# Recurrent heads: gate products from high and low parts, their split behind the next head's evictions, one filling gate half moved ahead

## The chip, the core and the metric

The kernel runs on one core of a Trainium2 chip, in one launch. The metric is the device time of that launch in microseconds (us). Five engines run programs of their own, each strictly in its order, and meet through semaphores: TensorE (PE in the profile; PEld is its weight loading), VectorE (DVE), ScalarE (ACT), GpSimd (POOL) and SyncE (SP, which issues most loads).

## What is computed

The reference is two transformer-like blocks on 1024 positions of width 1024, in float32. The change concerns one part of the second block, the gated linear recurrence of `rglru_direction`, in ten heads of 128 channels:

```python
xa = depthwise_conv(u_a, conv_a_w[l], conv_a_b[l], LRU_CONV // 2)
h_fwd = rglru_direction(xa, wa_f[l], ba_f[l], wx_f[l], bx_f[l], lam_f[l], False)
h_bwd = rglru_direction(xa, wa_b[l], ba_b[l], wx_b[l], bx_b[l], lam_b[l], True)
...
def rglru_direction(xc, wa, ba, wx, bx, lam, reverse):
    r = jax.nn.sigmoid(block_diag(xc, wa, ba).astype(jnp.float32))
    i = jax.nn.sigmoid(block_diag(xc, wx, bx).astype(jnp.float32))
    log_a = -LRU_C * r * jax.nn.softplus(-lam.astype(jnp.float32))
    a = jnp.exp(log_a)
    b_in = jnp.sqrt(-jnp.expm1(2.0 * log_a)) * (i * x32)
    _, h = lax.associative_scan(_lin_combine, (a, b_in), axis=1, reverse=reverse)
```

`block_diag` is block-diagonal: each head has its own 128x128 matrix, for each of four gates (r and i, forward and backward). So a head needs four products of a 128x128 matrix with its 128x1024 channels.

## The kernel before

Nearly all large products are made from split operands: a float32 matrix is written as a high part (ScalarE's copy to the 32-bit type fp32r) and a low part (the matrix less its high part, by GpSimd or VectorE), and three matmuls of such parts stand for one float32 product (the helper `three`, lines 401 to 403, which add hi*hi, hi*lo and lo*hi into one bank). Weights come in tiles of 128x1024: SP loads one into one of three staging buffers, ScalarE writes `weight_hi` (line 439), GpSimd `weight_lo` (line 461); five tiles are held at a time, and a tile's slot is filled again as soon as its last use is issued (`o.released()`).

There is no scheduler. One list of steps is written by hand (`order_lru` for this part), and each engine's program is that list, less the steps in which it has no part. So the place of a step in the list sets its place in the queue of each engine that takes part.

The recurrent heads run one behind the other, j from 0 to 9. For each j the list holds, in this order:

- `front(j + 1)` for the next head: `head_load` (SP loads the four matrices into `wbd`), `u` twice (24 matmuls of the projection each; ScalarE evicts each half into `raw`), a weight split for the slot that came free, `head_conv` (ScalarE's first tap, line 2661, then three taps on VectorE, line 2668, giving `xc`).
- `head_gate` eight times: TensorE multiplies `wbd` and `xc` in plain float32 (line 2681), ScalarE evicts with a sigmoid into `gt` (line 2692).
- `head_decay` for both directions: ScalarE's exponential `dc` and tanh `th` (lines 2701 and 2702), which read `gt`.
- `head_mid`: GpSimd squares `dc` (line 2708, called a2 below) and multiplies `gt` by `xc` (2710); VectorE makes `th` from a2 (2717, 2719).
- `gates.fill(1)`: one half (128x512, 24 matmuls) of the block's output gates, which have no bond to the heads and fill TensorE's time; ScalarE evicts it (line 854).
- `head_scan`: ScalarE's square root (2725), VectorE's product and scan for each direction (2732, 2740, 2742), into `hs`.
- `head_sum`: GpSimd adds both directions (2749) and issues the store (2751).
- `gates.fill(1)`: a second half, after which one more weight tile is split.

For the last head `window_front(0)`, the first projection of the pooling branch, stands in place of `front`. The pooling stage follows (`pool_out`, line 2834).

Of the kernel before, what the change touches and what calls it, by code (L numbers as in the profile page):

```python
# [7 lines left out]
F32 = mybir.dt.float32  # L8
F32R = mybir.dt.float32r
I32 = mybir.dt.int32  # L10
ALU = mybir.AluOpType
# [3 lines left out]
P = 128  # L15
# [162 lines left out]
class Memory:  # L178
# [5 lines left out]
    def put(self, name, shape, dtype=F32, right=False):  # L184
        n = int(np.prod(shape[1:])) * 4
        n = (n + 31) // 32 * 32
        self.names += 1
        if right:
            self.hi -= n
            at = self.hi  # L190
        else:
            at = self.lo
            self.lo += n
        assert self.lo <= self.hi, (name, self.lo, self.hi)
        return self.nc.alloc_sbuf_tensor_at(f"{name}_{self.names}", shape, dtype, offset=at)
# [203 lines left out]
def three(q, out, stat, mov, first, final, onto=False):  # L399

    q.matmul(out, stat[0], mov[0], start=first, stop=False, skip_group_check=onto)  # L401
    q.matmul(out, stat[0], mov[1], start=False, stop=False, skip_group_check=onto)  # L402
    return q.matmul(out, stat[1], mov[0], start=False, stop=final, skip_group_check=onto)  # L403
# [2272 lines left out]
def pe_head_gate(K, j, i, h):  # L2676
    pe, S, key = K.pe, K.S, ("lru", j, i, h)
    b = K.open(key)
    pe.wait_ge(S.wbd_load[j % 2], j)
    pe.wait_ge(S.dve_op, ("xc", j))  # L2680
    pe.q.matmul(b, K.wbd[j % 2][:, i, :], K.xc[j % 2][:, h * HALF:(h + 1) * HALF], start=True, stop=True).then_inc(*S.mm.up(key))


def act_head_gate(K, j, i, h):
# [219 lines left out]
def lay_out(K):  # L2904
# [80 lines left out]
            K.br[2] = [pair("br", [P, NL, HALF]), pair("br", [P, NP, HALF])]  # L2985
    m.lo, m.hi = end, high
    xn = [put("xn", [P, D], right=True) for _ in range(2)]
    below_xn = m.hi
    hT2 = pair("hT", [P, ND, S], right=True)

    m.lo, m.hi = low, below_xn
# [65 lines left out]
    m.lo = gates2_end  # L3057
    K.hs, K.xc = [put("hs", [P, S]) for _ in range(2)], [put("xc", [P, S]) for _ in range(2)]
    K.raw, K.raw2 = put("raw", [P, 16 + S + 16]), put("raw2", [P, 16 + S + 16])
    K.wbd, K.wpool = [put("wbd", [P, 4, P]) for _ in range(2)], put("wpool", [P, 2, GDIM])  # L3060
    K.sums = [put("sums", [P, 16 + S + 16]) for _ in range(2)]
    K.counts, K.pooled, K.yb2 = K.gt[0], K.dc, K.th

    K.norms = {
# [900 lines left out]
def order_lru(o, mix_norm):  # L3965
    gates = Gating(o, "gates2")
    gates.open()

    def block(c):
        w = o.take(gates.tile(c))  # L3970
        for h in range(NHALF):
            gates.one(c, h, w)
            yield
    blocks = [block(c) for c in range(GATES_AHEAD)]
    for n, b in enumerate(blocks):
        next(b)
        advance(mix_norm, (3, 0, 2, 0)[n])
    finish(mix_norm)
    for b in blocks:
        finish(b)  # L3980
    gates.done = 2 * GATES_AHEAD
    gates.close()
    o.handover()
    o.do("x2_stored")
    o.do("rates")
    gates.open()
    o.do("lru_edges")

    def front(j):
        o.do("head_load", j)  # L3990
        w = o.take(weight_block(o.io["w_in_2"][0], j * P))
        for h in range(NHALF):
            o.do("u", j, w, h)
        o.released()
        o.do("head_conv", j)
    def window_front(c):
        w = o.take(weight_block(o.io["w_in_2"][0], LW + c * P))
        for h in range(NHALF):
            o.do("pool_u", c, w, h)
        o.released()  # L4000
    front(0)
    for j in range(NL):
        if j + 1 < NL:
            front(j + 1)
        else:
            window_front(0)
        for i in range(4):
            for h in range(NHALF):
                o.do("head_gate", j, i, h)
        for d in range(2):  # L4010
            o.do("head_decay", j, d)
        for d in range(2):
            o.do("head_mid", j, d)
        gates.fill(1)
        for d in range(2):
            o.do("head_scan", j, d)
        o.do("head_sum", j)
        gates.fill(1)
    o.do("ya_stored")
    o.do("pool_edges")  # L4020
    for g in range(len(WINDOWS)):
        last = g + 1 == len(WINDOWS)
        if g == 0:
            o.do("counts_load", 0)
            o.do("wpool_load", 0)
            o.do("window_sums", 0)
            o.do("window_mean", 0)
            window_front(1)
            o.do("window_sums", 1)
            o.do("window_mean", 1)  # L4030
        if last:
            o.do("branch_fetch", 2, 0, 0, 0, NL)
            o.do("branch_fetch", 2, 0, 1, 0, NP - 2)
        gates.fill(2 * POOL_GATES[g])
        if last:
            gates.close()
            o.handover()
            for k in range(6):
                o.do("branch_load", 2, 0, 0, k)
        else:  # L4040
            window_front(2 * g + 2)
            o.do("counts_load", g + 1)
            window_front(2 * g + 3)
            o.do("window_sums", 2 * g + 2)
        for blk in (2 * g, 2 * g + 1):
            for h in range(NHALF):
                o.do("pool_out", blk, h)
            if not last:
                o.do("pool_store", blk)
        if not last:  # L4050
            o.do("wpool_load", g + 1)
            o.do("window_mean", 2 * g + 2)
            o.do("window_sums", 2 * g + 3)
            o.do("window_mean", 2 * g + 3)
    for k in range(6, NL):
        o.do("branch_load", 2, 0, 0, k)
    for k in range(NP):
        o.do("branch_load", 2, 0, 1, k)
    for blk in range(NP - 2, NP):
        o.do("pool_store", blk)  # L4060
# [44 lines left out]
def scalar_program(K, steps):  # L4105
    part = {"x_load": act_x_load, "square_in": act_square_in, "param": act_param, "weight": act_weight,
            "rstd": act_rstd, "turn": act_turn, "handover": act_handover, "gate": act_gate,
            "gates_close": act_gates_close, "z": act_z, "lora": act_lora, "sig_g": act_sig_g, "prep_kk": act_prep_kk,
            "prep_lora": act_prep_lora, "prep_decay": act_prep_decay, "prep_scale": act_prep_scale,
            "prep_length": act_prep_length, "tok": act_tok, "first": act_first, "level_w": act_level_w,  # L4110
            "local": act_local, "solve": act_solve, "bring": act_bring, "second": act_second, "compact": act_compact, "state": act_state, "y_turn": act_y_turn, "finish_1": act_finish_1,
            "finish_3": act_finish_3, "finish_4": act_finish_4, "compressed": act_compressed, "cnorm": act_cnorm, "cturn": act_cturn,
            "angles": act_angles, "q": act_q, "kv": act_kv, "exponent": act_exponent, "turn_p": act_turn_p,
            "output": act_output, "branch_load": act_branch_load, "gate_sum": act_gate_sum,
            "merge_rows": act_merge_rows, "split_hi": act_split_hi, "join": act_join,
            "act_split": act_act_split, "raw_first": act_raw_first, "conv_first": act_conv_first, "gelu": act_gelu, "down_rows": act_down_rows,
            "store_rows": act_store_rows, "ple_mix": act_ple_mix, "x2_stored": act_x2_stored, "rates": act_rates,
            "lru_edges": act_lru_edges, "u": act_u, "head_conv": act_head_conv, "head_gate": act_head_gate,
            "head_decay": act_head_decay, "head_scan": act_head_scan, "ya_stored": act_ya_stored,
            "pool_u": act_pool_u, "pool_store": act_pool_store, "yb_stored": act_yb_stored}  # L4120
    for kind, *what in steps:
        if kind in part:
            part[kind](K, *what)
# [21 lines left out]


def gpsimd_program(K, steps):
    part = {"param_load": pool_param_load, "param": pool_param, "weight": pool_weight, "gain": pool_gain,
            "handover": pool_handover, "gates_close": pool_gates_close, "rwkv_ready": pool_rwkv_ready,
            "level": pool_level,  # L4150
            "finish_4": pool_finish_4, "branch_load": pool_branch_load, "gate_sum": pool_gate_sum,
            "parts": pool_parts, "split_lo": pool_split_lo, "act_split": pool_act_split, "x2_stored": pool_x2_stored, "head_mid": pool_head_mid,
            "head_sum": pool_head_sum, "ya_stored": pool_windows_begin, "yb_stored": pool_yb_stored}
    for kind, *what in steps:
        if kind in part:
            part[kind](K, *what)
# [65 lines left out]
```

## Time and profile before

| what | value |
|---|---|
| median of 3 runs | 3463.3 us (3461.95 to 3465.99) |
| profiled execution | 3459.81 us, its span 3458.5 us |
| mean granted TensorE clock | 0.993 of full speed |
| PE busy | 3346.1 us, 97% of the span |
| DVE, ACT, POOL busy | 59%, 40%, 38% of the span |

The profile is of one execution. Its span is what the trace covers, and the time of that execution is 1.3 us longer. An engine's busy share is an average over all stages; the stage of the heads lies between 2046 and 2360 us of the span. A busy PE is one with some matmul in flight, and one matmul's duration in a row contains time that overlaps the next one; the distance between starts tells the rate.

### The profile page before, as it was taken

Reading aid. Unit: us, or ns where it says so; the run is one execution under the profiler, and the core shown is the slowest. Engines: PE = TensorE matmul, PEld = TensorE weight load, DVE = VectorE, ACT = ScalarE, POOL = GpSimd, SP = SyncE. Lnnn points to the kernel's source line nnn. Section 1 sums busy time; section 2 is a strip of 40 time slices with the busy share of each in tenths; the row PEclk is TensorE's granted clock in tenths of the full one; section 3 lists DMA queues with packets and bytes.
Section 4 is the critical chain, followed back from the end, with each engine's and each line's share of the span. In section 5 each row is a group of like instructions: output and inputs, shape, how many; then the busy total and the mean of one; then the engine's idle time right before and its main releaser. Section 6 shows DMA issues by size and latency. Waiting matters only on the chain.

```text
span 3458.5 us, 48890 instructions
## 1 busy us (share of the span) xinstructions
PE 3346.1 (97%) x19926; PEld 2718.4 (79%) x19926; DVE 2044.4 (59%) x2689; ACT 1390.3 (40%) x2361; POOL 1318.8 (38%) x698
## 2 busy tenths in 40 slices
PE   7999999999989999999999999999999999999999
PEld 6788888897668778878887777777788877777787
DVE  3655737427754743345555538886544588888554
ACT  4443434344533544431114447772233343443212
POOL 3212222110024444444442116662344365666542
PEclk9999999999999999999999999999999999999999
DMA  5101111020036344452222322222465423333522
GB/s 155 41 19 47 42 33 48 26 62 8 1 106 214 110 140 143 134 182 98 95 95 91 109 86 77 84 84 100 163 203 166 142 82 106 112 108 108 184 96 81
DMA packets 343792, 344.40 MB, mean 100 GB/s; under 512 B 14662, under 2 KB 263938, under 8 KB 343569
## 3 DMA queue, kind: packets, MB, share of 16 engines
q1 hardware_dynamic: 328960, 307.00, 28.1%
q10 hardware_dynamic: 11520, 25.17, 1.9%
q0 software_dynamic: 3088, 9.10, 0.7%
q8 instruction: 159, 2.61, 0.3%
q14 instruction: 65, 0.52, 0.1%
HBM read 268.86 MB, written 72.35 MB: 99 GB/s over the span
## 4 chain that ended last, share of the span: by engine, by line


## 5 line engine op out<-in xcount | busy, mean ns | idle before, releaser
L461 POOL TENSOR_TENSOR weight_lo<-stage,weight_hi 128x1024 fp32r<-128x1024 f32 (+4 forms) x269 | 627.9, 2341 | 981.5 <-ACT weight_hi L439 952.7
L2459 DVE TENSOR_TENSOR x<-x,psum 128x512 f32<-128x512 f32 x416 | 283.9, 687 | 281.7 <-PE psum L403 271.2
L439 ACT ACTIVATE weight_hi<-stage 128x1024 fp32r<-128x1024 f32 (+4 forms) x329 | 299.6, 925 | 328.5 <-PE psum L403 285.2
L401 PE MATMUL psum<-hT_hi,weight_hi 128*128 128x512 f32 x1024 | 411.0, 401 | 1.5 <-DVE hT_lo L654 1.5
L402 PE MATMUL psum<-hT_lo,weight_hi 128*128 128x512 f32 x1024 | 400.1, 391 | 0.0
L403 PE MATMUL psum<-hT_hi,weight_lo 128*128 128x512 f32 x1024 | 399.7, 390 | 0.0
L401 PE MATMUL psum<-weight_hi,act_hi 128*128 128x512 f32 x864 | 337.1, 390 | 5.3 <-POOL act_lo L2407 4.2
L403 PE MATMUL psum<-weight_hi,act_lo 128*128 128x512 f32 x864 | 336.9, 390 | 0.0
L402 PE MATMUL psum<-weight_lo,act_hi 128*128 128x512 f32 x864 | 336.8, 390 | 0.0
L461 POOL TENSOR_TENSOR weight_lo<-sum,weight_hi 128x512 fp32r<-128x512 f32 (+1 forms) x114 | 238.3, 2100 | 233.8 <-ACT weight_hi L439 233.7
L401 PE MATMUL psum<-T_hi,weight_hi 128*128 128x512 f32 x608 | 238.5, 392 | 18.5 <-POOL weight_lo L461 14.5
L402 PE MATMUL psum<-T_lo,weight_hi 128*128 128x512 f32 x608 | 236.7, 389 | 0.0
L403 PE MATMUL psum<-T_hi,weight_lo 128*128 128x512 f32 x608 | 236.7, 389 | 0.0
L401 PEld LDWEIGHTS psum<-hT_hi,weight_hi 128*128 128x128 f32 x1024 | 193.2, 189 | 50.6 <-issue 5.5
L402 PEld LDWEIGHTS psum<-hT_lo,weight_hi 128*128 128x128 f32 x1024 | 193.4, 189 | 43.0 <-issue 4.3
L403 PEld LDWEIGHTS psum<-hT_hi,weight_lo 128*128 128x128 f32 x1024 | 193.0, 188 | 40.8
L401 PEld LDWEIGHTS psum<-weight_hi,act_hi 128*128 128x128 f32 x864 | 162.6, 188 | 39.9 <-ACT out L2300 2.5
L2407 POOL TENSOR_TENSOR act_lo<-act_raw,act_hi 128x1024 fp32r<-128x1024 f32 x54 | 131.7, 2460 | 153.1 <-ACT act_hi L2398 153.1
L403 PEld LDWEIGHTS psum<-weight_hi,act_lo 128*128 128x128 f32 x864 | 162.6, 188 | 34.1
L402 PEld LDWEIGHTS psum<-weight_lo,act_hi 128*128 128x128 f32 x864 | 162.5, 188 | 33.8
L401 PE MATMUL psum<-B_hi,weight_hi 128*128 128x512 f32 x456 | 179.9, 394 | 8.1 <-ACT kept L2289 3.7
L402 PE MATMUL psum<-B_lo,weight_hi 128*128 128x512 f32 x456 | 178.8, 392 | 0.0
(421 smaller groups left out, 7095.5 us busy)
## 6 DMA issues: line engine op xcount, KB each, us to landing
stage<-in_w_up SPq DMA_DIRECT2D x66, 512.0 KB, 4.3
stage<-in_w_in SPq DMA_DIRECT2D x64, 512.0 KB, 4.0
act_raw<-scratch_act SPq DMA_DIRECT2D x54, 512.0 KB, 5.3
stage<-in_w_ffn_up SPq DMA_DIRECT2D x48, 512.0 KB, 4.7
scratch_gates<-gate ACTq DMA_DIRECT2D x64, 256.0 KB, 2.0
gs<-scratch_gates SPq DMA_DIRECT2D x64, 256.0 KB, 3.1
stage<-in_w_out SPq DMA_DIRECT2D x32, 512.0 KB, 4.5
scratch_act<-out SPq DMA_DIRECT2D x64, 256.0 KB, 4.8
```

The costliest lines, as they stand in the source:

```text
L401: q.matmul(out, stat[0], mov[0], start=first, stop=False, skip_group_check=onto)
L402: q.matmul(out, stat[0], mov[1], start=False, stop=False, skip_group_check=onto)
L403: return q.matmul(out, stat[1], mov[0], start=False, stop=final, skip_group_check=onto)
L439: a.q.activation(hi[:, part], src, ACT.Copy).then_inc(*S.w_hi.up(w))
L461: g.q.tensor_tensor(lo[:, part], src, hi[:, part].bitcast(F32), ALU.subtract).then_inc(*S.w_lo_pool.up(w))
L2407: g.q.tensor_tensor(lo, K.act_raw[i % 4][:, :], hi.bitcast(F32), ALU.subtract).then_inc(*S.act_lo.up((f, i)))
L2459: v.q.tensor_tensor(dst, dst, K.bank(key), ALU.add).then_inc(*S.x.up(("f", f, g, t, n)))
```

## The change

The gate products are made by `three` from `wbd_hi`, `wbd_lo`, `xc_hi` and `xc_lo`. A new step `head_split` makes these: ScalarE copies `xc` and `wbd` to the high parts, GpSimd subtracts for the low parts. The step for head j stands in `front(j + 1)`, behind the weight split and ahead of `head_conv`. The `fill` that stood behind `head_mid` stands ahead of the gates.

```diff
 def pe_head_gate(K, j, i, h):
     pe, S, key = K.pe, K.S, ("lru", j, i, h)
     b = K.open(key)
-    pe.wait_ge(S.wbd_load[j % 2], j)
-    pe.wait_ge(S.dve_op, ("xc", j))
-    pe.q.matmul(b, K.wbd[j % 2][:, i, :], K.xc[j % 2][:, h * HALF:(h + 1) * HALF], start=True, stop=True).then_inc(*S.mm.up(key))
+    pe.wait_ge(S.act_op, ("wbd_hi", j))
+    pe.wait_ge(S.pool_op, ("wbd_lo", j))
+    at = slice(h * HALF, (h + 1) * HALF)
+    three(pe.q, b, (K.wbd_hi[:, i, :], K.wbd_lo[j % 2][:, i, :]), (K.xc_hi[:, at], K.xc_lo[:, at]), True, True).then_inc(*S.mm.up(key))
+
+
+def act_head_split(K, j):
+    a, S = K.a, K.S
+    a.wait_ge(S.dve_op, ("xc", j))
+    if j:
+        a.wait_ge(S.mm, ("lru", j - 1, 3, 1))
+    a.q.activation(K.xc_hi[:, :], K.xc[j % 2][:, :], ACT.Copy).then_inc(*S.act_op.up(("xc_hi", j)))
+    a.wait_ge(S.wbd_load[j % 2], j)
+    a.q.activation(K.wbd_hi[:, :, :], K.wbd[j % 2][:, :, :], ACT.Copy).then_inc(*S.act_op.up(("wbd_hi", j)))
+
+
+def pool_head_split(K, j):
+    g, S = K.g, K.S
+    g.wait_ge(S.act_op, ("xc_hi", j))
+    g.q.tensor_tensor(K.xc_lo[:, :], K.xc[j % 2][:, :], K.xc_hi[:, :].bitcast(F32), ALU.subtract).then_inc(*S.pool_op.up(("xc_lo", j)))
+    g.wait_ge(S.act_op, ("wbd_hi", j))
+    g.q.tensor_tensor(K.wbd_lo[j % 2][:, :, :], K.wbd[j % 2][:, :, :], K.wbd_hi[:, :, :].bitcast(F32), ALU.subtract).then_inc(
+        *S.pool_op.up(("wbd_lo", j)))
...
         for h in range(NHALF):
             o.do("u", j, w, h)
         o.released()
+        if j:
+            o.do("head_split", j - 1)
         o.do("head_conv", j)
...
             front(j + 1)
         else:
             window_front(0)
+            o.do("head_split", j)
+        gates.fill(1)
         for i in range(4):
...
         for d in range(2):
             o.do("head_mid", j, d)
-        gates.fill(1)
         for d in range(2):
             o.do("head_scan", j, d)
```

`wbd_lo` lies in place over `wbd`; `xc_hi`, `xc_lo` and `wbd_hi` get room of their own.

Where the new instructions land is shown at two places. First GpSimd's queue over one head in steady state, before: the sum of the head just ended, its store, two weight splits, then the four operations of the next head's `head_mid`.

```order
L2749 TENSOR_TENSOR hs_258<-hs_258,hs_259 128x1024
L2751 DMA scratch_ya<-hs_258 128x1024
L461 TENSOR_TENSOR weight_lo_66<-stage_52,weight_hi_65 128x1024
L461 TENSOR_TENSOR weight_lo_62<-stage_53,weight_hi_61 128x1024
L2708 TENSOR_TENSOR gt_248<-dc_252 128x1024
L2710 TENSOR_TENSOR gt_249<-gt_249,xc_261 128x1024
L2708 TENSOR_TENSOR gt_250<-dc_253 128x1024
L2710 TENSOR_TENSOR gt_251<-gt_251,xc_261 128x1024
```

The same stretch of GpSimd's queue with the change:

```order
L2769 TENSOR_TENSOR hs_258<-hs_258,hs_259 128x1024
L2771 DMA scratch_ya<-hs_258 128x1024
L461 TENSOR_TENSOR weight_lo_66<-stage_52,weight_hi_65 128x1024
L461 TENSOR_TENSOR weight_lo_62<-stage_53,weight_hi_61 128x1024
L2698 TENSOR_TENSOR xc_lo_271<-xc_261,xc_hi_270 128x1024
L2700 TENSOR_TENSOR wbd_lo_273<-wbd_265,wbd_hi_269 128x512
L2728 TENSOR_TENSOR gt_248<-dc_252 128x1024
L2730 TENSOR_TENSOR gt_249<-gt_249,xc_261 128x1024
L2728 TENSOR_TENSOR gt_250<-dc_253 128x1024
L2730 TENSOR_TENSOR gt_251<-gt_251,xc_261 128x1024
```

The two subtractions of the new step stand behind the sum of the head before and the two weight splits, and ahead of the squares that need this head's gates.

The other place is ScalarE's queue between two heads, with its waits, with the change (before, the two rows at lines 2690 and 2692 and the two of the filling gate, 854 and 859, are not between `weight_hi` and the gates' sigmoids).

```order
L439 ACTIVATE weight_hi_61<-stage_53 128x1024 [waits stage_load1]
L2690 ACTIVATE xc_hi_270<-xc_261 128x1024
L2692 ACTIVATE wbd_hi_269<-wbd_265 128x512 [waits wbd_load1]
L2661 ACTIVATE xc_260<-raw_262,param_50 128x1024 [waits pool_op_done,act_evac_done]
L854 ACTIVATE gate_246<-psum,param_50 128x512 [waits gates2_store0,mm_done]
L859 DMA scratch_gates<-gate_246 128x512 [waits gate_ready]
L2712 ACTIVATE gt_248<-psum,param_50 128x512 [waits mm_done] x2
```

ScalarE makes the next head's first tap (line 2661) later by the two copies, and one of its two filling evictions has moved ahead of the sigmoids. On TensorE the eight gate products of a head, 8 float32 matmuls before, are 24 matmuls of parts, and 24 matmuls of a filling half stand ahead of them and no longer behind them.

## Rows read from the trace of the kernel before

**Rows 1.** Windows: PE, PEld, DVE, ACT, POOL busy us; clock; DMA share; GB/s.
```profile
2150.00:2180.00 30.00, 30.00 (x117) 21.64 (x116) 26.79 (x12) 23.00 (x27) 19.88 (x9) 1.00 0.25 79
```
**Rows 2.** Timeline of PE: start us, us, then idle before. First head's gates.
```profile
2029.77 0.39 PE L401 MATMUL psum<-hT_hi,weight_hi 128*128 128x512 f32 x1
...
2062.18 0.39 PE L403 MATMUL psum<-hT_hi,weight_lo 128*128 128x512 f32 x1
2062.41 7.03 PE L2681 MATMUL psum<-xc,wbd 128*128 128x512 f32 x16
...
2069.50 0.39 PE L402 MATMUL psum<-hT_lo,weight_hi 128*128 128x512 f32 x1
```
**Rows 3.** Timeline of PE's weight loads: first of the gates of two heads.
```profile
2119.48 0.41 PEld L2681 LDWEIGHTS psum<-xc,wbd 128*128 128x128 f32 x2
...
2148.12 0.41 PEld L2681 LDWEIGHTS psum<-xc,wbd 128*128 128x128 f32 x2
```
**Rows 4.** Timeline of POOL: first head's weight split, then one steady head.
```profile
2064.33 2.35 POOL L461 TENSOR_TENSOR weight_lo<-stage,weight_hi 128x1024 fp32r<-128x1024 f32 x1 [5.92 <-ACT weight_hi L439]
...
2151.02 2.35 POOL L2749 TENSOR_TENSOR hs<-hs,hs 128x1024 f32<-128x1024 f32 x1 [8.79 <-DVE hs L2742]
...
2154.28 5.77 POOL L461 TENSOR_TENSOR weight_lo<-stage,weight_hi 128x1024 fp32r<-128x1024 f32 x2
2160.00 2.89 POOL L2708 TENSOR_TENSOR gt<-dc 128x1024 f32<-128x1024 f32 x1
...
2179.66 2.36 POOL L2749 TENSOR_TENSOR hs<-hs,hs 128x1024 f32<-128x1024 f32 x1 [8.79 <-DVE hs L2742]
```
**Rows 5.** Timeline of DVE: second head's taps, then a steady head's.
```profile
2065.49 4.92 DVE L2668 SCALAR_TENSOR_TENSOR xc<-raw,param,xc 128x1024 f32<-128x1024 f32 x3 [3.35 <-ACT xc L2661]
...
2151.68 9.46 DVE L2668 SCALAR_TENSOR_TENSOR xc<-raw,param,xc 128x1024 f32<-128x1024 f32 x3 [0.74 <-ACT xc L2661]
2162.99 3.33 DVE L2717 SCALAR_TENSOR_TENSOR th<-gt,th 128x1024 f32<-128x1024 f32 x1 [1.85 <-POOL gt L2708]
```
**Rows 6.** Timeline of ACT: last square root of a head, next head's tanh.
```profile
2172.72 1.06 ACT L2725 ACTIVATE th<-th 128x1024 f32<-128x1024 f32 x1 [3.01 <-DVE th L2719]
...
2187.29 1.14 ACT L2702 ACTIVATE th<-gt,neg 128x1024 f32<-128x1024 f32 x1
```
**Rows 7.** Timelines of PE, ACT and POOL in the last head.
```profile
2320.18 7.03 PE L2681 MATMUL psum<-xc,wbd 128*128 128x512 f32 x16
...
2327.25 0.69 ACT L2692 ACTIVATE gt<-psum,param 128x512 f32<-128x512 f32 x1 [0.17 <-PE psum L2681]
...
2331.52 1.90 POOL L2708 TENSOR_TENSOR gt<-dc 128x1024 f32<-128x1024 f32 x1 [0.60 <-ACT th L2702]
...
2350.20 2.40 POOL L2749 TENSOR_TENSOR hs<-hs,hs 128x1024 f32<-128x1024 f32 x1 [8.79 <-DVE hs L2742]
```
**Rows 8.** Groups by line and shape from 1500 us on: subtractions and a copy.
```profile
L461 POOL TENSOR_TENSOR weight_lo<-stage,weight_hi 128x512 fp32r<-128x512 f32 x22 | 48.2, 2193 | 0.0
L2080 POOL TENSOR_TENSOR merged_lo<-gs,merged_hi 128x512 fp32r<-128x512 f32 x16 | 20.7, 1297 | 121.9 <-ACT merged_hi L2073 121.9
...
L439 ACT ACTIVATE weight_hi<-stage 128x1024 fp32r<-128x1024 f32 x155 | 162.2, 1054 | 289.3 <-PE psum L403 269.2 <-DMA stage<-in_w_out 6.9 <-ACT gate L854 5.6
```
**Rows 9.** PE and PEld behind an idle stretch, and its clock by stretches.
```profile
2473.45 0.47 PE L401 MATMUL psum<-br_hi,weight_hi 128*128 128x512 f32 x1 [2.08 <-DVE br_lo L2025]
...
2475.71 0.33 PEld L403 LDWEIGHTS psum<-br_hi,weight_lo 128*128 128x128 f32 x1
2476.14 0.33 PEld L401 LDWEIGHTS psum<-br_hi,weight_hi 128*128 128x128 f32 x1
...
2475.00:2476.00 1.00, 1.00 (x3) 0.80 (x3) 1.00 (x1) 0.00 (x0) 1.00 (x1) 0.50 1.05 412
...
2478.00:2479.00 1.00, 1.00 (x6) 0.83 (x5) 1.00 (x3) 0.00 (x0) 0.34 (x1) 1.00 0.06 25
```
**Rows 10.** Timeline of PE at the pooling stage's first products.
```profile
2371.39 7.11 PE L2834 MATMUL psum<-dc,wpool 128*128 128x512 f32 x16 [0.65 <-DVE dc L2825]
```

More of the change, by code:

```diff
@@ L2987, in lay_out @@
     xn = [put("xn", [P, D], right=True) for _ in range(2)]
-    below_xn = m.hi
+    below_xn = xn_at = m.hi
     hT2 = pair("hT", [P, ND, S], right=True)
@@ L3059, in lay_out @@
     K.raw, K.raw2 = put("raw", [P, 16 + S + 16]), put("raw2", [P, 16 + S + 16])
+    wbd_at = m.lo
     K.wbd, K.wpool = [put("wbd", [P, 4, P]) for _ in range(2)], put("wpool", [P, 2, GDIM])
     K.sums = [put("sums", [P, 16 + S + 16]) for _ in range(2)]
+    K.wbd_hi = put("wbd_hi", [P, 4, P], F32R)
+    assert m.lo <= lows_at
+    m.lo = xn_at
+    K.xc_hi, K.xc_lo = put("xc_hi", [P, S], F32R), put("xc_lo", [P, S], F32R)
+    m.lo = wbd_at
+    K.wbd_lo = [put("wbd_lo", [P, 4, P], F32R) for _ in range(2)]
     K.counts, K.pooled, K.yb2 = K.gt[0], K.dc, K.th
@@ L4117, in scalar_program @@
             "store_rows": act_store_rows, "ple_mix": act_ple_mix, "x2_stored": act_x2_stored, "rates": act_rates,
-            "lru_edges": act_lru_edges, "u": act_u, "head_conv": act_head_conv, "head_gate": act_head_gate,
+            "lru_edges": act_lru_edges, "u": act_u, "head_conv": act_head_conv, "head_gate": act_head_gate, "head_split": act_head_split,
             "head_decay": act_head_decay, "head_scan": act_head_scan, "ya_stored": act_ya_stored,
@@ L4147, in gpsimd_program @@
 def gpsimd_program(K, steps):
-    part = {"param_load": pool_param_load, "param": pool_param, "weight": pool_weight, "gain": pool_gain,
+    part = {"head_split": pool_head_split, "param_load": pool_param_load, "param": pool_param, "weight": pool_weight, "gain": pool_gain,
             "handover": pool_handover, "gates_close": pool_gates_close, "rwkv_ready": pool_rwkv_ready,
```

## The prediction

> **What bounds the kernel now.** I first read the windows of the heads' stage: TensorE is busy for all of 30.00 us at full clock, and VectorE, ScalarE and GpSimd for 26.8, 23.0 and 19.9 us of it [rows 1]. Three engines that are this full beside a full TensorE call for a second look: who waits for whom. The timeline of TensorE shows an unbroken stream. Ahead of the first gates 144 matmuls of parts start between 2029.77 and 2062.18, 0.2266 us apart, and the 16 records of eight float32 products last from 2062.41 until the filling half's second matmul at 2069.50; less that half's first matmul, 6.86 us [rows 2]. The gates of the next heads begin 28.64 us apart [rows 3]. That is just TensorE's work for one head: 6.86 us, and 96 matmuls of parts (two halves of a projection, two filling halves) in 21.75 us.
>
> The timelines of the other engines show a second bound of the same length, and it is the one that matters here. GpSimd starts a head's sum when VectorE's last scan has ended, stores, splits two weight tiles from 2154.28 and comes to the next head's a2 at 2160.00; its next sum starts at 2179.66, 28.64 us after the one before, and its only long wait is 8.79 us for the scan [rows 4]. VectorE's first work on a2 starts at 2162.99, released by GpSimd [rows 5]. From a2 on VectorE works without a gap to the scan, and the scan lets the next sum start. So scan, sum, weight splits, a2, scan is a closed chain without slack. What keeps it at 28.64 us is that the head's gates are not in it: ScalarE has this head's tanh at 2187.29 + 1.14 = 2188.43, just before GpSimd needs it, since TensorE made the gates while the previous head was still in its scans [rows 6].
>
> **What the change takes away.** Eight float32 products of 6.86 us become 24 matmuls of parts at 0.2266 us, 5.44 us: 1.42 us a head, 14.2 us over ten. TensorE's work for a head falls to 27.2 us.
>
> **What it adds, and where.** ScalarE gets a 128x1024 copy (1.05 us by the weights' copy) and one of 128x512, some 0.6 us as half of it and a fixed part [rows 8]. They lie behind the projection's evictions; GpSimd is then still waiting for the scan or splitting weights, so they cost nothing by themselves. If that cover went, they would cost 1.7 us a head. GpSimd gets xc_lo (128x1024) and wbd_lo (128x512). Their price alone would be small. Their place is not: in GpSimd's queue they stand behind the previous head's sum and behind both weight splits, and ahead of a2. The gates wait for wbd_lo, a2 waits for the gates. What ran beside the previous head's scans, the gates and their evictions, now starts only after them. The order of one head becomes a single chain, which I add up from one start of the gates to the next:
>
> - 24 matmuls: 23 x 0.2266 us and the last one's 0.39 us make 5.6 us [rows 2]; at the clock that I expect, 1.6 us more (below): 7.2 us.
> - Last eviction to a2: in the last head, where nothing else stood in the way, the eviction began at 2327.25 and a2 at 2331.52, 4.27 us; with a hop from TensorE, 4.3 us [rows 7]. All eight evictions stand ahead of the tanh in ScalarE's queue, so the whole set of gates is in the chain.
> - a2 to the sum: 2331.52 to 2350.20, 18.7 us [rows 7].
> - Sum to the weight splits: 2151.02 to 2154.28, 3.3 us [rows 4].
> - Two weight splits and xc_lo: the two took 5.72 us (2154.28 to 2160.00) while VectorE's taps ran; at that rate three take 8.6 us [rows 4].
> - wbd_lo: between 1.30 and 2.19 us by the two rows of 128x512 subtractions [rows 8]. By then the three taps, of some 3 us each beside the splits [rows 5], are over; I take 1.3 us, and 0.1 us for hops: 1.4 us.
>
> Together 43.5 us where there were 28.64. TensorE has 27.2 us of work in it at full clock and idles for about 14 us in each head. The filling half ahead of the gates doesn't cover this: the wait is longer than all the other work that a head has.
>
> **The clock.** Such waits have a price of their own. TensorE resumed at 2473.45 after an idle stretch of 2.08 us; in 2475 to 2476 the granted clock was 0.50 of full speed, the 1.2 GHz level, with weight loads 0.43 us apart in place of 0.23, and from 2478 it was 1.00 [rows 9]. So I expect the first gates of each head at half speed. From 2475 to 2478 about 3 us were slow; with the partly slow ends I take 3.4 us, in which 8 matmuls run where 15 would: 7 x 0.2266 = 1.6 us. The bounds are none, and the whole set at 0.43 us, 4.7 us.
>
> The Trainium skill, page "TensorE: Matmul & The Clock Gate", section "HAM oscillation — how this bites in real kernels", describes this: a loop that leaves TensorE waiting in every turn starts every turn at the low clock. The trace agrees with its one such wait (0.50 after 2.08 us); by the page alone each turn would start slowly, which the sum already holds.
>
> **Blocking between VectorE and GpSimd.** Three taps took 4.92 us when GpSimd had little to do and 9.46 us beside its splits [rows 5], and two splits took 5.72 us instead of 2 x 2.35 us [rows 4]. This is in the 8.6 us above. Without it three would take 7.05 us.
>
> The Trainium skill, page "SBUF — State Buffer", section "Who interferes with whom", has a stricter rule: a two-input VectorE operation and a GpSimd operation that reads SBUF exclude each other for a whole instruction. If VectorE were first each time, xc_lo and each split would wait for a tap of about 1.3 us; the three would take about 11 us and the kernel some 20 us more than I forecast. The split's 2.86 us beside the taps shows about 0.5 us each, so I stay with the row.
>
> **The ends.** First head: GpSimd ends a weight split at 2064.33 + 2.35 = 2066.68 [rows 4]; xc_lo (2.9 us beside the next head's taps) and wbd_lo (1.3 us) end near 2071.0, where the gates began at 2062.41 [rows 2]: 8.6 us late, 5.4 us of them spent on the filling half. Last head: no taps beside the splits, so 7.1 us in place of 8.6, and the turn is 42.0 us. The last gates come later by 8.6 + 8 x (43.5 - 28.64) + (42.0 - 28.64) = 140.9 us. Behind them the chain to the pooling products is as long as before, to 0.2 us (7.2 + 4.3 = 11.5 us to a2, before 2331.52 - 2320.18 = 11.3) [rows 7]. TensorE waited 0.65 us there [rows 10]; now it has 5.4 us less to fill the time, waits some 6 us and meets the low clock once more, 1.6 us. Sum: 142.7 us.
>
> On the profiled execution that is 3459.8 + 142.7 = 3602.5 us; the median of the runs lay 3.5 us above it, so I forecast 3605 us for a median. About 0.2% is what a measurement of this kernel can tell from no change.
>
> **Rivals.**
>
> - *A single chain (the forecast)*: chance 82%. With no slow clock, no blocking and the low price of wbd_lo the turn is 40.3 us and the kernel about 3575 us; with all gates at the low clock and 2.2 us for wbd_lo, 47.4 us and about 3644 us.
> - *GpSimd has room* (the other side): its 8.79 us of waiting in each head would hold both subtractions (some 4.2 us), TensorE would stay full, and the 14.2 us would be gained: 3449 us. This decides if wbd_lo comes within the 21.75 us of other matmuls between two sets of gates. For it speaks that GpSimd is 38% busy. Against it: the 8.79 us lie ahead of the sum, the subtractions behind it. 4%.
> - *Only GpSimd's chain grows*: the two subtractions lengthen the old chain by some 4.2 us a head, and the gates still overlap the scans: ten times 4.2 us on the median, 3505 us. It would need a2 not to depend on late gates, and it reads `dc`, made from them. 5%.
> - *The low clock stays*: TensorE is granted its lower level for most of each turn. The gates then cost 10.3 us, and the other 96 matmuls 41 us, more than the chain leaves them, so that TensorE would bound a turn of about 51 us: some 3680 us. Rows 9's recovery within about 3 us of work speaks against it, since 22 us of work lie unbroken behind the gates. 6%.
> - *No change to speak of*: the gain and some waits cancel. 3%.
>
> **How the numbers follow.** The forecast is the first case. Its bounds, a little widened at the low end, give 3570 to 3645 us, which leaves the other cases, 18%, outside. Faster by over 0.2%: 4%. Within 0.2%: 3%. Slower: 93%.
>
> **What would show it.** In the changed profile the gates should start about 43 us apart, with TensorE idle for some 14 us ahead of them, released by GpSimd's `wbd_lo`; the clock should be at its low level at their start; GpSimd should go from the sum through two splits and two subtractions without a gap, and then wait about 11 us for the tanh. DVE and ACT should have the same work a head, spread thinner. I am wrong if TensorE stays full in this stage, if the wait ends with another engine, or if the starts are under 38 us apart.

## The result and the profile after

| what | before | changed |
|---|---|---|
| median, us (runs) | 3462.7 (4) | 3609.1 (4), 3607.7 to 3611.4 |
| ratio to before | 1 | 1.0424, 95% interval 1.0410 to 1.0439 |
| profiled execution, us | 3459.8 | 3611.4, its span 3610.1 |
| mean granted TensorE clock | 0.993 | 0.970 |

The change costs 146 us; the forecast was 3605 us, 4 us less than was measured, inside 3570 to 3645. The table of waits of the changed kernel (us in total, times, longest) shows the place in one line, the first of TensorE's list:

```profile
PE psum L401 <- POOL wbd_lo L2700: 134.4, 10, 14.8
```

Windows of the same kernel (columns as in [rows 1]) show what became of TensorE's unbroken stream, and the granted clock at the start of one head's gates:

```profile
2180.00:2210.00 30.00, 15.22 (x61) 12.21 (x60) 20.73 (x10) 11.32 (x14) 17.41 (x8) 0.73 0.25 79
...
2206.00:2207.00 1.00, 0.34 (x1) 0.37 (x2) 0.00 (x0) 0.00 (x0) 0.52 (x1) 0.50 0.00 0
2210.00:2211.00 1.00, 1.00 (x3) 0.78 (x3) 0.00 (x0) 0.41 (x2) 0.00 (x0) 0.50 0.00 0
2211.00:2212.00 1.00, 1.00 (x5) 0.76 (x4) 0.00 (x0) 0.82 (x2) 0.00 (x0) 0.96 0.00 0
2212.00:2213.00 1.00, 1.00 (x6) 0.84 (x5) 0.00 (x0) 1.00 (x2) 0.00 (x0) 1.00 0.00 0
```

TensorE is busy for 15.2 of 30 us where [rows 1] had 30.0, and no other engine is full in its place: VectorE, ScalarE and GpSimd all do less in the stretch than before. That is how a chain looks, in contrast to a busy engine that sets the pace.

One turn of the chain, from the timelines of all engines in the changed kernel, in order of time:

```profile
2162.36 0.29 PEld L401 LDWEIGHTS psum<-xc_hi,wbd_hi 128*128 128x128 f32 x1 [15.17 <-issue]
...
2174.44 1.89 POOL L2728 TENSOR_TENSOR gt<-dc 128x1024 f32<-128x1024 f32 x1 [12.19 <-ACT th L2722]
...
2193.11 2.35 POOL L2769 TENSOR_TENSOR hs<-hs,hs 128x1024 f32<-128x1024 f32 x1 [8.79 <-DVE hs L2762]
2195.23 1.31 DVE L2668 SCALAR_TENSOR_TENSOR xc<-raw,param,xc 128x1024 f32<-128x1024 f32 x1 [2.20 <-ACT xc L2661]
2196.38 5.64 POOL L461 TENSOR_TENSOR weight_lo<-stage,weight_hi 128x1024 fp32r<-128x1024 f32 x2
2201.98 3.31 POOL L2698 TENSOR_TENSOR xc_lo<-xc,xc_hi 128x1024 fp32r<-128x1024 f32 x1
2205.26 1.26 POOL L2700 TENSOR_TENSOR wbd_lo<-wbd,wbd_hi 128x512 fp32r<-128x512 f32 x1
2206.63 0.29 PEld L401 LDWEIGHTS psum<-xc_hi,wbd_hi 128*128 128x128 f32 x1 [15.17 <-issue]
2206.66 0.77 PE L401 MATMUL psum<-xc_hi,wbd_hi 128*128 128x512 f32 x1 [14.78 <-POOL wbd_lo L2700]
2207.23 0.63 PE L402 MATMUL psum<-xc_lo,wbd_hi 128*128 128x512 f32 x1
...
2208.32 0.69 ACT L2712 ACTIVATE gt<-psum,param 128x512 f32<-128x512 f32 x1 [12.54 <-PE psum L403]
...
2520.86 4.49 PE L2854 MATMUL psum<-dc,wpool 128*128 128x512 f32 x5 [4.81 <-DVE dc L2845]
```

Read down the left column: gates at 2162.36, a2 at 2174.44, sum at 2193.11, splits at 2196.38 to 2206.5, the next gates at 2206.63. GpSimd's, TensorE's and ScalarE's steps in this list follow one another; only VectorE's tap (line 2668) runs beside a split. GpSimd waits 12.19 us for the tanh, where before its only long wait was the one for the scan [rows 4]; ScalarE waits 12.54 us for the gates' first bank. The last row is the pooling product that answers to [rows 10]: its wait grew from 0.65 to 4.81 us.

### The profile page after: what moved, and what is told of

Same layout as the page of the kernel before. It is cut to its first block, busy times and chain, and to the rows that moved or that the text cites. A ratio compares the mean times of both kernels' runs of the same rounds, so it can differ in the third digit from the quotient of the medians.

```text
span 3610.1 us, 49080 instructions
## 1 busy us (share of the span) xinstructions
PE 3359.1 (93%) x20006; PEld 2750.9 (76%) x20006; DVE 2040.1 (57%) x2689; ACT 1398.5 (39%) x2371; POOL 1353.0 (37%) x718
## 4 chain that ended last, share of the span: by engine, by line
```

## The experiments

All medians stand beside runs of the kernel before on the same chip; those gave medians of 3462.5 to 3462.9 us. "A turn" is the distance between the starts of two heads' gates, by the weight loads: 28.64 us before, 44.3 us in the changed kernel.

### One part alone

**e2_fill_ahead_alone**, the kernel before with only the filling half moved:

```diff
+        gates.fill(1)
         for i in range(4):
...
             o.do("head_mid", j, d)
-        gates.fill(1)
```

> The kernel before with only the filling half moved ahead of the float32 gates; no split. Single chain: the gates need nothing from the previous head's scan, so TensorE stays full in the heads and the turn is 28.6 to 29.5 us; the tail lacks 5.4 us of filling work: 3466 to 3480 us. Rival (the half's new place is what slows the changed kernel): most of the 146 us, 3560 us or more.

3469.1 us, ratio 1.0018 (1.0008 to 1.0028). Turns stay at 28.64 us; TensorE waits 5.0 us at the pooling products, since one half fewer lies behind the last gates. This part is worth 6 us of the 146.

**e5_split_unread**, the changed kernel with the gates in plain float32 again. The split is made, but nothing reads it, so that TensorE doesn't wait for it; `wbd_lo` no longer lies over `wbd` but in the room of a later stage's buffer (an edit not shown here):

```diff
-    pe.wait_ge(S.pool_op, ("wbd_lo", j))
...
-    three(pe.q, b, (K.wbd_hi[:, i, :], K.wbd_lo[j % 2][:, i, :]), (K.xc_hi[:, at], K.xc_lo[:, at]), True, True).then_inc(*S.mm.up(key))
+    pe.wait_ge(S.wbd_load[j % 2], j)
+    pe.wait_ge(S.dve_op, ("xc", j))
+    pe.q.matmul(b, K.wbd[j % 2][:, i, :], K.xc[j % 2][:, h * HALF:(h + 1) * HALF], start=True, stop=True).then_inc(*S.mm.up(key))
```

> The changed kernel's order with the split made in its place but not read: the gates are the float32 products of before (wbd_lo is written to a buffer of the later pooling stage). Single chain: with the gates out of it, only GpSimd's two subtractions lengthen the old chain of 28.65 us, to about 33 us a turn; with the moved half's 6 us at the end 3500 to 3515 us. So of the 146 us about 40 would be GpSimd's extra work and the rest the gates' wait for it. Rival (GpSimd's extra work alone is what costs): 3590 us or more. Rival (GpSimd has room): 3469 us, as with the half moved alone.

3500.6 us, ratio 1.0113 (1.0097 to 1.0130). One turn is 32.3 us by GpSimd's a2:

```profile
2212.56 1.92 POOL L2727 TENSOR_TENSOR gt<-dc 128x1024 f32<-128x1024 f32 x1
...
2244.85 1.91 POOL L2727 TENSOR_TENSOR gt<-dc 128x1024 f32<-128x1024 f32 x1
```

That is the old chain, longer by the two subtractions. TensorE's own 28.64 us a head, with the float32 gates, lie below it and don't set the pace. So 38 us of the 146 are the extra work in GpSimd's queue and the moved half; the other 108 us come only from the gates' waiting for it. This is the division that the forecast and its rival "only GpSimd's chain grows" (3505 us) disputed.

**e1_fill_back**, the changed kernel with the half behind `head_mid` again (the diff of e2 turned round):

> The changed kernel with the filling gate half back behind head_mid; the split stays where the change put it. Single chain (scan, sum, two weight splits, xc_lo, wbd_lo, gates, tanh, a2, scan): the filling half isn't in that chain, so the gates stay 44.3 us apart and TensorE's wait ahead of them grows from 14.8 to about 20 us; only the tail, where the half fills TensorE's 4.8 us again, gives some back: 3600 to 3611 us. Rival (the moved half delays each head's gates by its 5.4 us): 39 us a turn, about 3555 us.

3594.3 us, ratio 1.0373 (1.0358 to 1.0389): 15 us faster than the changed kernel, neither what I expected nor the rival's figure. TensorE still waits 123.9 us for `wbd_lo`, and a turn is 42.3 us on average. The difference is in the timelines of VectorE and GpSimd:

```profile
2187.81 9.53 DVE L2668 SCALAR_TENSOR_TENSOR xc<-raw,param,xc 128x1024 f32<-128x1024 f32 x1 [3.05 <-ACT xc L2661]
2188.10 4.64 POOL L461 TENSOR_TENSOR weight_lo<-stage,weight_hi 128x1024 fp32r<-128x1024 f32 x2
2192.70 2.34 POOL L2698 TENSOR_TENSOR xc_lo<-xc,xc_hi 128x1024 fp32r<-128x1024 f32 x1
2195.00 1.25 POOL L2700 TENSOR_TENSOR wbd_lo<-wbd,wbd_hi 128x512 fp32r<-128x512 f32 x1
```

One tap lasts 9.53 us, from 0.29 us ahead of GpSimd's first split until 1.1 us behind its last subtraction, where in the changed kernel the tap that starts 1.15 us ahead of the split took 1.31 us. Here VectorE stands still and GpSimd's three large subtractions take 6.98 us by their rows, not 8.95 as in the changed kernel. VectorE is not in the chain at that time, GpSimd is: so 2 us a turn are gained by which of the two comes first (from the first split to the gates it is 8.26 us in each of e1's turns, 10.25 in the changed kernel's first eight).

### The clock

**e4_keep_warm** and **e8_warm_later_heads** put useless matmuls, whose result nothing reads, ahead of the filling half's own, in all heads and in heads 1 to 9:

```diff
-        gates.fill(1)
+        gates.fill(1, 20)                 # e4: 20 x 3 more matmuls
...
+        gates.fill(1, 20 if j else 0)     # e8
```

> The changed kernel with 60 useless matmuls (13.6 us at full clock) ahead of the filling half that precedes each head's gates; they write a bank that the half then overwrites. Single chain: TensorE's wait ahead of the gates shrinks from 14.8 to about 1 us, the gates then run at full clock, and the turn falls from 44.3 to about 42.1 us: 3585 to 3595 us, faster than the changed kernel in spite of 136 us of added work. Rival (the low clock costs nothing in the chain): 3605 to 3611 us. Rival (TensorE's own work bounds the heads): 3745 us.

> The useless matmuls ahead of the filling half only for heads 1 to 9, not for head 0, where TensorE has no long wait for them to fill. If the low clock costs about 1.8 us a turn and head 0 paid some 11 us for its useless matmuls: 3590 to 3596 us. If the clock is not what the useless matmuls changed: 3603 us or more.

e4 took 3603.7 us (ratio 1.0405, 1.0390 to 1.0421), e8 3594.0 us (1.0382, 1.0367 to 1.0398); the mean granted clock was 0.993 in both. e4 missed because head 0 has no long wait to fill: its gates began at 2083.9 in place of 2074.4. In e8 turns are 42.5 us against 44.3: from the gates to a2 it is 10.07 us in place of some 12.1, and the three splits with their hop take 0.2 us more (10.42 against 10.25). The low clock therefore costs some 2 us a turn, of which 1.8 us come back in e8, 15 us in all, a tenth of the loss.

### The split at another place

**e3_split_early** makes head j+1's split behind `head_mid` of head j, ahead of the previous sum in GpSimd's queue (and the half at its old place), so that the new step no longer stands behind that sum:

```diff
-            o.do("head_split", j - 1)
...
             o.do("head_mid", j, d)
+        if j + 1 < NL:
+            o.do("head_split", j + 1)
+        gates.fill(1)
```

**e7_split_at_scans** puts it behind `head_scan`, **e6_weights_deferred** is e3 with the two weight splits behind that split too (`o.released(2)` there; none behind the projections).

> Gate products from parts, but head j+1's split stands right behind head j's head_mid, ahead of the sum of head j and of the weight splits; the filling half is back behind it. Single chain: the split falls into GpSimd's wait for the scans (8.8 us), the gates again run beside the scans; the turn is bound by the old chain of 28.65 us with some blocking on VectorE, 28.6 to 29.8 us: 3460 to 3477 us, TensorE at full clock. Rival (the price of GpSimd's extra work, wherever it stands): 4.5 us a head more, about 3508 us. Rival (TensorE's saving counts now): 3449 us.

> The early split moved a little later, from behind head_mid to behind head_scan (still ahead of the sum): GpSimd then subtracts beside VectorE's scans and no longer beside its maximum and first product. If the 3.2 us a turn that the early split cost came from blocking of those operations, most of it goes and the turn is 28.7 to 30 us: 3463 to 3480 us. If the scans are blocked as well, 31 to 32.5 us: 3490 to 3510 us.

> The early split (right behind head_mid), and the two weight splits of a head also moved from behind the sum to behind that split. Chain: scan, sum, a2 no longer holds the 5.7 us of weight splits, so the turn is bound by TensorE's 27.2 us if the weight splits fit beside VectorE's work: 3449 us. Rival (GpSimd and VectorE exclude each other, and the weight splits now fall on VectorE's chain from a2 to the scan): 28.5 to 31 us a turn, 3463 to 3490 us.

| | median, us | ratio (95%) | steady turn, us |
|---|---|---|---|
| e3 | 3499.6 | 1.0105 (1.0090 to 1.0120) | 31.8 |
| e7 | 3500.6 | 1.0114 (1.0099 to 1.0129) | 31.8 |
| e6 | 3497.6 | 1.0104 (1.0089 to 1.0119) | 31.3 |

The place of the split is what mattered: each is over 100 us faster than the changed kernel. But all three stop 35 to 38 us above the kernel before, wherever GpSimd's work stands. Of e3's theories the forecast (3460 to 3477 us) failed; nearest was the rival by which the work costs 4.5 us a head wherever it stands (3508 us), where 3.2 us a turn were measured. e7 came out as its second theory had it, with the scans blocked as well (3490 to 3510 us). e6 is above both of its theories. VectorE's timeline in e3, where GpSimd's two subtractions run from 2219.82 to 2224.85 and nothing of GpSimd from there to 2231.78:

```profile
2211.97 3.34 DVE L2737 SCALAR_TENSOR_TENSOR th<-gt,th 128x1024 f32<-128x1024 f32 x1 [4.22 <-POOL gt L2728]
...
2220.98 2.75 DVE L2739 TENSOR_SCALAR th<-th 128x1024 f32<-128x1024 f32 x1
2223.65 2.28 DVE L2752 TENSOR_TENSOR th<-th,gt 128x1024 f32<-128x1024 f32 x1
2225.97 2.29 DVE L2760 TENSOR_TENSOR_SCAN hs<-dc,th 128x1024 f32<-128x1024 f32 x1
2228.18 1.20 DVE L2752 TENSOR_TENSOR th<-th,gt 128x1024 f32<-128x1024 f32 x1
2229.42 2.29 DVE L2762 TENSOR_TENSOR_SCAN hs<-dc,th 128x1024 f32<-128x1024 f32 x1
```

Timelines of VectorE and GpSimd in e6:

```profile
2219.25 2.72 DVE L2739 TENSOR_SCALAR th<-th 128x1024 f32<-128x1024 f32 x1
...
2223.05 7.72 POOL L461 TENSOR_TENSOR weight_lo<-stage,weight_hi 128x1024 fp32r<-128x1024 f32 x2
2224.22 4.36 DVE L2760 TENSOR_TENSOR_SCAN hs<-dc,th 128x1024 f32<-128x1024 f32 x1
2228.50 3.36 DVE L2752 TENSOR_TENSOR th<-th,gt 128x1024 f32<-128x1024 f32 x1
```

and in e7:

```profile
2195.05 3.52 POOL L2698 TENSOR_TENSOR xc_lo<-xc,xc_hi 128x1024 fp32r<-128x1024 f32 x1 [3.93 <-ACT xc_hi L2690]
2196.30 3.35 DVE L2752 TENSOR_TENSOR th<-th,gt 128x1024 f32<-128x1024 f32 x1
2198.53 2.25 POOL L2700 TENSOR_TENSOR wbd_lo<-wbd,wbd_hi 128x512 fp32r<-128x512 f32 x1
2199.69 3.24 DVE L2762 TENSOR_TENSOR_SCAN hs<-dc,th 128x1024 f32<-128x1024 f32 x1
...
2224.01 0.69 DVE L2739 TENSOR_SCALAR th<-th 128x1024 f32<-128x1024 f32 x1
```

The same operations last 0.69 us (L2739), 1.20 us (L2752) and 2.29 us (the scan) when GpSimd does nothing. Beside a subtraction each grows by 1 to 2 us, and GpSimd's subtractions grow too (two in 7.72 us, 4.64 us alone in e1). So the two engines hold each other off, and much of VectorE's busy time is not work.

What bounds the turn is not the same in the three. In e3 and e7 VectorE still has a gap of 4.22 us in each turn, ended by a2: the old chain through sum, weight splits and a2 is still closed there, and longer by what its operations lose beside the subtractions. In e6 VectorE has no gap for a whole turn. Counted by the shortest time of each in that run, a turn's operations are 14.6 us on VectorE and 19.7 us on GpSimd; their sum, an estimate of 34 us, is a little above the turn of 31.3 us, so that hardly any of it overlaps. In e6 the sum of both is what comes near the bound.

### Room for GpSimd

If that is so, taking work off GpSimd must help. ScalarE can square `dc`:

```diff
+    a.wait_ge(S.act_op, ("tanh", j, d))
+    a.q.activation(K.gt[2 * d][:, :], K.dc[d][:, :], ACT.Square).then_inc(*S.act_op.up(("a2", j, d)))
...
-    g.q.tensor_tensor(K.gt[2 * d][:, :], K.dc[d][:, :], K.dc[d][:, :], ALU.mult).then_inc(*S.pool_op.up(("a2", j, d)))
```

**e10_square_act_alone** is this edit on the kernel before, **e9_early_square_act** on e3, **e11_deferred_square_act** on e6. **e12_both_full** is e11 with two steps moved: head 0's split to behind its own `front`, and the filling half ahead of the gates for heads 0 to 8, which saves ScalarE one 1.28 us change between its sets of functions a head.

> The kernel before, with a2 by ScalarE and nothing else. TensorE's float32 gates keep its turn at 28.64 us, so nothing is gained: 3458 to 3468 us. If the chain of the other engines was the only bound before: 3450 us or less.

> The early split, and a2 (the square of dc) by ScalarE in place of GpSimd. If VectorE and GpSimd exclude each other so far that the sum of their work bounds the turn of 31.8 us of the early split, 3.8 us less on GpSimd give 27.5 to 29 us a turn: 3450 to 3468 us. If instead GpSimd's order (sum, weight splits, then head_mid) is the bound: the turn loses only what stood between the splits and VectorE's first work, about 2 us: 29.8 us, 3470 to 3485 us. If ScalarE becomes the bound by its two squares: 31 us or more, 3490 us.

> The early split with the weight splits behind it, and a2 by ScalarE. If the sum of VectorE's and GpSimd's work bounds the turn (31.3 us with a2 on GpSimd), 3.8 us less give 27.3 to 28.5 us: 3449 to 3463 us. If ScalarE's chain (square root, next gates, tanh, squares) becomes the bound: 29 us or more, 3466 us or more.

> The kernel of the run before (weights' splits deferred, square on ScalarE) with the filling half ahead of the gates again in heads 0 to 8 and with head 0's split ahead of head 1's front. Its mean turn was 28.1 us by the starts of the gates, its best turns 27.20 us, TensorE's own work for a head; its last turns were 28.2 us, where ScalarE's queue closed a chain of its own, and head 0 cost 6.5 us of waiting for wbd_lo. With the filling half's eviction standing ahead of the sigmoids ScalarE changes between its sets of functions once less in a head, 1.28 us less work a turn. Theory that ScalarE's chain was the last bound: all turns come to 27.2 us, head 0 waits little, and of the 14.2 us that TensorE saves some 5 to 12 us appear: 3450 to 3458 us, faster than both kernels. Rival, VectorE and GpSimd with their mutual exclusion are the bound by now whatever ScalarE does: turns stay at 28 us or go above, and the time is 3460 us or more.

| | median, us (11 runs each) | ratio (95%) | turns, us |
|---|---|---|---|
| e10 | 3461.8 | 0.9996 (0.9987 to 1.0005) | 28.64 |
| e9 | 3462.8 | 0.9999 (0.9990 to 1.0008) | 28.9, then 27.2 to 28.4 |
| e11 | 3463.9 | 1.0004 (0.9995 to 1.0013) | 29.8, then 27.2 to 27.3, the last two 28.2 |
| e12 | 3461.0 | 0.9996 (0.9987 to 1.0005) | 27.2, one 27.8, the last 25.6 (no half ahead of its gates) |

On the kernel before, the square's move does nothing (e10: TensorE is the bound as well). On e3 and e6 it takes 34 to 37 us away. On e3 the move also takes a2 out of the closed chain, so that e9 alone doesn't tell the chain from the sum; e11, made from e6, is the test of the sum. (e11's nine turns are 27.7 us on average, not 28.1 as the expectation of e12 has it.) In e12 TensorE has its full stream again at the 27.2 us of work that the change leaves it, and even so the kernel is no faster than before by what a measurement can tell. Of the 12.8 us that nine shorter turns should bring, 8.8 are left at the last gates and 4.9 at the pooling products. Windows, then VectorE and GpSimd in the last head, then TensorE at the last gates and at the pooling products, of e12:

```profile
2200.00:2230.00 30.00, 30.00 (x134) 24.85 (x133) 29.72 (x13) 25.06 (x29) 24.01 (x10) 1.00 0.25 79
```

```profile
2329.29 2.42 POOL L461 TENSOR_TENSOR weight_lo<-stage,weight_hi 128x1024 fp32r<-128x1024 f32 x1
2329.55 10.30 DVE L2736 SCALAR_TENSOR_TENSOR th<-gt,th 128x1024 f32<-128x1024 f32 x1 [3.67 <-ACT gt L2724]
2331.66 4.75 POOL L2730 TENSOR_TENSOR gt<-gt,xc 128x1024 f32<-128x1024 f32 x2
2336.39 2.38 POOL L461 TENSOR_TENSOR weight_lo<-stage,weight_hi 128x1024 fp32r<-128x1024 f32 x1
```

```profile
2314.28 0.47 PE L401 MATMUL psum<-xc_hi,wbd_hi 128*128 128x512 f32 x1 [1.48 <-POOL wbd_lo L2700]
...
2369.39 1.19 PE L2853 MATMUL psum<-dc,wpool 128*128 128x512 f32 x1 [4.72 <-DVE dc L2844]
```

VectorE is at 29.72 of 30 us (30.1 us of operations in a turn of 27.2, counted as above). The last gates start at 2314.28, after a wait of 1.5 us for `wbd_lo` and 5.9 us before [rows 7]'s 2320.18, or 8.8 us if one allows for the 2.9 us by which this execution was late ahead of the stage (its weight split of [rows 4]'s time comes at 2058.91, in the profile of before at 2056.01). Then one product of VectorE lasts 10.30 us, until GpSimd's four operations are done; the pooling products start at 2369.4, only 4.9 us earlier by the same allowance. TensorE has run out of work 4.7 us before that, and meets the lower level (0.50 in the windows from 2369 to 2374). What is left is 1.5 us of the median, inside its uncertainty. e12's theory was right for the turns and wrong for the time.

The Trainium skill, page "SBUF — State Buffer", section "Who interferes with whom", says that a two-input VectorE operation and a GpSimd operation that reads SBUF exclude each other for a whole instruction, and that the order of issue decides who is blocked. On the exclusion the 9.53 and 10.30 us rows agree, and there the loser waits for four GpSimd operations in a row. On the order the rows don't decide: in e1 the tap that lost began 0.29 us ahead of the split.

## Why the prediction was right

- **The mechanism** held: gates, a2, scans, sum, splits, gates is one chain, TensorE waits in every head (13.4 us on average; predicted some 14), `wbd_lo` ends the wait, GpSimd then waits 12.2 us for the tanh (predicted 11). e5 shows that the wait and not the work is the larger part; e3, e6 and e7 show that it goes with the place of the split.
- **The turn** was 43.5 us by the sum, 44.25 us measured over the first eight. By terms: a2 to sum 18.67 (18.7), sum to splits 3.27 (3.3), splits and hop 10.25 (10.0), gates to a2 12.08 (11.5). The last is the clock: ten matmuls ran at the 1.2 GHz level, 0.43 us apart from 2206.66 to 2211.07, which costs 2.1 us where I took 1.6. In the nine heads behind the first, 3.1 to 4.4 us were slow.
- **The ends**: first gates at 2074.46, 12.05 us after [rows 2]'s; this execution was 3.0 us late ahead of the stage already (the same weight split at 2059.05 against 2056.01), so 9.0 us (8.6). The last turn was 42.35 us (42.0). The last gates are 147.6 us late by the same allowance (140.9), nearly all of the difference being nine turns at 0.7 us. The wait at the pooling products was 4.8 us (6).
- **The whole**: profiled execution against profiled execution, 151.6 us less those 3.0 make 148.6, against a sum of 142.7. Of the 0.75 us by which a turn is longer than the sum, the clock's term is 0.5 us too small (2.1 in place of 1.6 us) and the splits' term 0.25 us.
- **What was luck**: the median is 4 us above the forecast, the profiled execution 8.9 us above its own (3611.4 against 3602.5). The forecast added 3.5 us because the median before lay so far above the profiled execution; in the changed kernel it lies 2.3 us below, and that hides more than half of the miss. The clock's term, too, rested on less than the prediction says: [rows 9] is not the one wait of its kind. In the same trace an idle stretch of the same length was followed by 6 us at full clock, and so were others of 1.8 to 2.0 us:

```profile
3208.99 0.47 PE L401 MATMUL psum<-weight_hi,act_hi 128*128 128x512 f32 x1 [2.07 <-POOL act_lo L2407]
...
3209.00:3215.00 6.00, 6.00 (x27) 4.94 (x27) 3.63 (x4) 2.77 (x3) 6.00 (x3) 1.00 0.32 96
```

  That the gates start at the low level after waits of 13 to 15 us is shown by the changed kernel (0.50), and e8, where the wait is 1.4 us, has them at full clock; [rows 9] doesn't show it.
- **The blocking**: the rows' 8.6 us for three splits (8.95 measured) was nearer than the 11 us of the stricter rule. But the rule's mechanism is real; in this kernel GpSimd lost 2 us by it. e1 shows the other order, in which GpSimd loses nothing (6.98 us).
- **The rivals** with room on GpSimd (3449 us), with only GpSimd's chain grown (3505 us) and with a lasting low clock (3680 us) are excluded by the 134.4 us row, by e5 and by the clock's return to 1.00 within 6 us.

Left open: whether another order in the last head of e12 would keep its gain. It wasn't tried. Nor is it shown what ordered tap and split differently in e1 than in the changed kernel; the rows show only that the tap began 0.86 us closer to the split.

## What to carry to other kernels

When a step is moved into the queue of an engine with room, ask what stands ahead of it in that queue and whether it depends on the results of the turn before: here a 4.6 us pair of subtractions behind the sum tied two overlapping halves of a loop into one chain and cost 108 us, more than seven times the 14.2 us that TensorE was to save. When several engines close at the same turn length, speeding up one gains nothing until the others have room, and then the end of the loop, with its last waits and the clock behind them, can still eat the gain. Before you take VectorE or GpSimd for an engine with room, add up the operations of both in the stretch: here 34 us of them, each at its shortest, made a turn of 31.3 us.

## What was unexpected of the hardware

- VectorE and GpSimd held each other off in every kind of operation that VectorE has in this stage, scans included: a blocked scan took 3.24 to 4.39 us and 2.29 us alone, a one-input `tensor_scalar` mostly 2.3 to 2.8 us against 0.69 us.
- One loss can last through four operations (9.53 and 10.30 us for a VectorE operation of 1.3 us). In e10 this befalls a tap in eight of the ten heads (9.6 to 10.8 us) and costs nothing, since TensorE sets the pace. The starts alone don't tell which engine loses: a tap that began 0.29 us ahead of a split lost to four operations (e1), one that began 0.20 us behind a split lost to that one only (changed kernel, 3.24 us).
- After a wait of 13 to 15 us TensorE ran 3.1 to 4.4 us of matmuls at the lower clock, in nine heads of ten, though some 22 us of work at the full level lay between two waits.
